# Near products of a chunked scan with a compact output matrix of 64 columns, spread into the padded one by ScalarE

## The chip, the cores and the metric

The kernel runs on one core of one Trainium2 chip, in one launch. The metric is the device time of that execution in microseconds (us); shorter is better. Five engines work side by side, each with its own list of instructions: TensorE (PE in the profile, its weight loads PEld), VectorE (DVE), ScalarE (ACT), GpSimd (POOL) and SyncE (SP), which here only starts DMAs. They wait for each other through semaphores, counters that an instruction raises when it ends and that another engine waits on.

## What is computed

A trunk of two layers on 256 tokens of width 2048, all in float32. Layer 1 is a forgetting attention with a projection before and behind it and is not touched. Layer 0 runs a state-space group (S5) and a differential attention side by side on one projection:

```
h = rms(x, e_norm);  u, z_s5, q, k, v, z_da = split(h @ e_w_in)
# S5: 64 groups of 16 channels, each with 64 complex states
xr, xi = einsum('blgh,gph->blgp', u, B)            # into the states
h_t = a * h_(t-1) + x_t                            # associative_scan over 256 tokens
y = einsum(h_re, c_re) - einsum(h_im, c_im) + d*u
y = gelu(y);  y_s5 = y * sigmoid(y @ w_glu + b_glu) * silu(z_s5)
y_da = diff_attention(q, k, v) * silu(z_da)
x = x + concat(y_s5, y_da) @ e_w_out
```

## The kernel before, in words

**Projections.** Weights stream from memory in units of two 128-row blocks by 512 columns, through a ring of four buffers. To keep float32 accuracy at the fast rate of the float32r type, ACT copies each unit `raw` into a rounded high part `wh` (split_hi, L942), DVE forms the rest `wl` (split_lo, L950), and TensorE multiplies high by high, low by high and high by low (rows_unit, L452 to L454, 12 products of 512 columns per unit). split_hi of a unit waits until TensorE has used the unit four before it (unit_used), split_lo for hi_done, TensorE for lo_done.

**Order.** The order on each engine is written out in the source. The 16 units of two column chunks make a step of slots 0 to 15. In a slot every engine first does the S5 operations and the attention operations assigned to it by the tables of slot numbers at the top of the file, and then (TensorE: before them) its part of the unit; ACT and DVE work three units ahead (LEAD). S5 is done in four batches i = 0 to 3 of 16 groups; slot 0 of batch i is the first slot of step i+1, and negative slots reach back into the step before. The attention of head pair i-1 runs in the same step. Slots below are those of the batch.

**The scan.** The 256 tokens are cut into chunks of HOP = 4. Within a chunk everything is done by a small matrix per tile (a tile is two groups, TB = 8 tiles per batch); between chunks 64 states are carried by a hardware scan on DVE.
- s5_powers (DVE) fills `ba`: B times powers of a. s5_far (DVE, slots -6 and -1, one call for each part r) fills `ca`: C times powers of a, five powers k of 32 output columns. Two groups share a tile: rows 0 to 63 hold group 0 and rows 64 to 127 group 1. `ca` is a padded matrix: group g has its 16 columns at 16g of every 32, and the others are zeros, written once at the start (by POOL's memset, semaphore zeros). Products L1607 (two of 128x640), then L1614 adds or subtracts them half by half into `ca`, and L1618 raises ca_done.
- s5_skip (DVE) fills diag_d, the diagonal of d, with 128 columns.
- s5_turn (TensorE, slot 0) transposes `ba` (L663), and ACT copies it out (L1034, xin_sb).
- s5_near (TensorE, slots 0 and 4, h = 0 and 1): four tiles each, three products into 32 rows of a PSUM bank: L675 and L676 multiply 32 columns of `ba` by 128 columns of `ca` (real and imaginary part), L677 adds the diagonal over 32 columns. It waits for xin_sb, and with h = 0 for ca_done and dd_done. Then ACT (s5_near, slots 1 and 5, L1045) copies the result into `near` four times, each time shifted into another 32 rows (near_sb).
- s5_in_x (TensorE, slots 3 and 6, L691) brings the inputs in, rotate_in and rotate_out (DVE, slots 4, 5 and 8) turn and scan, s5_out_near and s5_out_y (TensorE, slots 7 and 9, L698 and L706, y_ps) form the outputs, and ACT's s5_gelu (L1054, slots 10, 11, 11 and 13) takes them out.

**The attention beside it.** Scores L520 (TensorE) of one head and component wait for sc_max, which DVE (score_in, L1764 to L1767) raises once it has read the scores before them. ACT's exponentials L1176 follow, DVE combines, TensorE transposes (L533, slot 4), ACT copies out (L1184, pt_sb, slot 5) and TensorE multiplies by the values (L546 to L548, slot 5). In a slot, S5 comes ahead of the attention on every engine.

Of the kernel before, what the change touches and what calls it, by code (L numbers as in the profile page):

```python
# [11 lines left out]
ALU = mybir.AluOpType  # L12
# [3 lines left out]
P = 128  # L16
# [57 lines left out]
IN_SLOT, OUT_SLOT = [4, 8], [5, 8]  # L74
GELU_SLOT, HIGH_SLOT = [10, 11, 11, 13], 14
# [51 lines left out]
def build(nc, d, out_dram):  # L127
    ctx = ExitStack()
    with ctx:
# [52 lines left out]
        def small_at(a, n):  # L182
# [26 lines left out]
        g_half = small_at(166, 2)  # L209

# [14 lines left out]
        diag_d = carve("scr", 2, P)  # L225
        used["scr"] += 256
# [33 lines left out]
        ca_t = [flat[:, 3072 + 640 * k:3072 + 640 * (k + 1)].rearrange("p (i k h) -> p i k h", i=TB, k=5)  # L260
                for k in range(2)]
        ba_t = [x.rearrange("p r n -> p (r n)").rearrange("p (i s h) -> p i s h", i=TB, s=HOP) for x in prod]
        phc = carve("scr", 4, GP + 2)
        with nc.sbuf_tensor("mg", [P, TB, NCH], F32) as mg:
# [46 lines left out]
        ba_done, ca_done, dd_done, steps_done = (sem(n) for n in  # L311
            ("ba_done", "ca_done", "dd_done", "steps_done"))
# [120 lines left out]
        def _(pe):  # L433
# [232 lines left out]
            def s5_near(i, h):  # L666

                pe.wait_ge(xin_sb, 4 * i + (3 + h))
                if h == 0:
                    pe.wait_ge(ca_done, i + 1)  # L670
                    pe.wait_ge(dd_done, i + 1)
                o = (xb, yb)[h]
                for e in range(TH):
                    t, at = TH * h + e, e * P
                    nc.tensor.matmul(o[0:32, at:at + P], ba[:, 0, t, 0:32], ca[:, 0, t, 0:P], start=True, stop=False)  # L675
                    nc.tensor.matmul(o[0:32, at:at + P], ba[:, 1, t, 0:32], ca[:, 1, t, 0:P], start=False, stop=False)  # L676
                    mm = nc.tensor.matmul(o[0:32, at:at + 32], ident[:, 32 * e:32 * e + 32],  # L677
                                          diag_d[:, h, 32 * e:32 * e + 32], start=False, stop=True)
                mm.then_inc(near_ps, 1)
# [21 lines left out]
            def s5_out_y(i, h):  # L701
                pe.wait_ge(h_done, 2 * i + (h + 1))
                for e in range(TH):
                    t = TH * h + e
                    for r in range(2):
                        mm = nc.tensor.matmul(xb[:, t * NCH + 1:(t + 1) * NCH], ca[:, r, t, 32:32 + P],  # L706
                                              hst[h][:, r, e * NCH:(e + 1) * NCH - 1], start=False, stop=r == 1,
                                              skip_group_check=True)
                if h:
                    mm.then_inc(y_ps, 1)  # L710
# [244 lines left out]
        def _(act):  # L955
# [81 lines left out]
            def s5_near(i, h):  # L1037

                act.wait_ge(near_ps, 2 * i + (h + 1))
                if h == 0:  # L1040
                    act.wait_ge(y_ps, i) if i else act.wait_ge(zeros, 2)
                src = (xb, yb)[h][0:32, :].rearrange("p (i n) -> p i n", i=TH)
                for s in range(HOP):
                    at = 32 * (HOP - 1 - s)
                    ins = nc.scalar.activation(near[32 * s:32 * s + 32, TH * h:TH * h + TH, at:P], src[:, :, 0:P - at], ACT.Copy)  # L1045
                ins.then_inc(near_sb, 1)

# [13 lines left out]
            def s5(n, s):  # L1061

                for i in range(DA_PAIRS):
                    at = s5_at(n, s, i)
                    if TAB_SLOT[1] + 1 == at:
                        table(i)
                    for k in range(4):
                        if T_SLOT[k] + 1 == at:
                            s5_turned(i, k)
                    for h in range(2):  # L1070
                        if NEAR_SLOT[h] + 1 == at:
                            s5_near(i, h)
                    for k in range(HOP):
                        if GELU_SLOT[k] == at:
                            s5_gelu(i, k)
                    if HIGH_SLOT == at:
                        s5_high(i)
# [347 lines left out]
        def _(dve):  # L1425
# [126 lines left out]
            def gains():  # L1552
# [4 lines left out]
                v.tensor_scalar(g_qk[1][:, 0:1], g_qk[1][:, 0:1], float(HD) ** -0.5, None, ALU.mult)  # L1557
                link(v.memset(g_half, 0.0))
# [36 lines left out]
            def s5_far(i, r):  # L1595
# [13 lines left out]
                times(ca_t[0], r, 0)  # L1609
                link(times(ca_t[1], 1 - r, 1))  # L1610
                for half in range(2):
                    at = slice(64 * half, 64 * half + 64)
                    o = ca[at, r, :, :].rearrange("p i (k h) -> p (i k) h", k=5)[:, :, 16 * half:16 * half + 16]
                    ins = v.tensor_tensor(o, *(x[at].rearrange("p i k h -> p (i k) h") for x in ca_t),  # L1614
                                          ALU.subtract if r else ALU.add)
                link(ins)
                if r:
                    v.memset(junk1[:, 2:3], 0.0).then_inc(ca_done, 1)  # L1618
# [30 lines left out]
            def s5_skip(i):  # L1649
                if i:  # L1650
                    dve.wait_ge(near_ps, 2 * i)
                for c in range(2):
                    ins = v.tensor_scalar(diag_d[:, c, :], ident, d_col[:, 2 * i + c:2 * i + c + 1], None, ALU.mult)
# [7 lines left out]
            def rotate_in(i, h):  # L1661
                dve.wait_ge(x_ps, 2 * i + (h + 1))
                if h == 0:
                    dve.wait_ge(tab_done, i + 1)
                    dve.wait_ge(y_ps, i)
                a1, a2 = prod
# [9 lines left out]
            def rotate_out(i, h):  # L1676
                a1, a2 = prod
# [459 lines left out]
```

## Time and profile before

| | us |
|---|---|
| median of 3 runs | 985.17 (984.67 to 985.78) |
| the profiled execution | 983.37 |
| its span | 981.6 |
| TensorE busy | 966.3 (98% of the span) |
| TensorE weight loads | 828.8 (84%) |
| DVE busy | 629.2 (64%) |
| ACT busy | 572.5 (58%) |
| POOL busy | 94.4 (10%) |

The four batches of the scan lie between about 111 and 370 us of the span. TensorE ran at its full granted clock throughout. A matmul's row in the timeline shows its start and a modelled end; the time that one costs in a stream is the distance from start to start. "Idle before" names the releaser that came last by the profile, which need not be the one that was waited for when an instruction waits for several.

### The profile page before, as it was taken

The page shows a single profiled execution, that of the slowest core. Times are in us where ns is not written, and L with a number is a line of the kernel's source. Part 1 is how long each engine was busy: PE and PEld are TensorE (multiplying, and loading weights), DVE is VectorE, ACT ScalarE, POOL GpSimd, SP SyncE. Part 2 cuts the span into 40 slices and gives each one's busy share as a digit, 9 for nine tenths or more (in the row PEclk, how much of TensorE's full clock was granted, in tenths as well). Part 3 has the DMA queues.
Part 4 walks back from the last instruction along what each step waited for, and adds up shares of the span by engine and source line. Part 5 has one row for each costly group of instructions (what it writes and reads, how often), then busy time and mean ns, then how long its engine had stood idle before and what let it go on. Part 6 is the DMA issues. An engine that isn't in the chain of part 4 may idle for free.

```text
span 981.6 us, 14482 instructions
## 1 busy us (share of the span) xinstructions
PE 966.3 (98%) x5315; PEld 828.8 (84%) x5315; DVE 629.2 (64%) x995; ACT 572.5 (58%) x934; POOL 94.4 (10%) x92
## 2 busy tenths in 40 slices
PE   8999999999999999999999999999999999999998
PEld 7988888788787999888888888888888888888887
DVE  5687898898889755665554654555455545555553
ACT  5697758767567655654445465446545654565332
POOL 2101002011021010000002200220022002200000
PEclk9999999999999999999999999999999999999999
DMA  8874444334433447565799985667999956654662
GB/s 287 207 205 151 151 134 135 119 107 129 141 110 117 129 129 264 166 202 188 173 168 175 168 180 166 177 184 151 173 155 175 196 163 177 180 167 151 215 215 86
DMA packets 113858, 163.63 MB, mean 167 GB/s; under 512 B 19221, under 2 KB 54154, under 8 KB 113546
## 3 DMA queue, kind: packets, MB, share of 16 engines
q1 hardware_dynamic: 99504, 159.67, 61.7%
q10 hardware_dynamic: 14298, 3.22, 1.6%
q8 instruction: 35, 0.57, 0.2%
q14 instruction: 21, 0.17, 0.1%
HBM read 160.76 MB, written 2.10 MB: 166 GB/s over the span
## 4 chain that ended last, share of the span: by engine, by line
PE 90%; DVE 5%; ACT 4%; issue 1%; DMA 0%; SPq 0%; ACTq 0%
PE bank L452 22%; PE bank L454 22%; PE bank L453 22%; PE bank L479 4%; PE bank L480 4%; PE bank L481 4%; ACT uz L1054 2%; PE bank L706 1%; PE bank L691 1%; ACT wh L942 1%; DVE wl L950 1%; PE bank L595 1%; PE bank L520 1%; PE bank L586 1%; PE bank L698 1%
## 5 line engine op out<-in xcount | busy, mean ns | idle before, releaser
L950 DVE TENSOR_TENSOR wl<-raw,wh 128x1024 fp32r<-128x1024 f32 x295 | 361.1, 1228 | 273.0 <-ACT wh L942 271.8
L942 ACT ACTIVATE wh<-raw 128x1024 fp32r<-128x1024 f32 x295 | 310.1, 1057 | 170.0 <-PE bank L454 124.6
L452 PE MATMUL bank<-wh,xh 128*128 128x512 f32 x768 | 309.1, 403 | 0.0
L454 PE MATMUL bank<-wh,xl 128*128 128x512 f32 x768 | 300.3, 391 | 0.0
L453 PE MATMUL bank<-wl,xh 128*128 128x512 f32 x768 | 299.2, 390 | 0.0
L454 PEld LDWEIGHTS bank<-wh,xl 128*128 128x128 f32 x768 | 144.1, 188 | 31.7
L453 PEld LDWEIGHTS bank<-wl,xh 128*128 128x128 f32 x768 | 144.7, 188 | 26.9
L452 PEld LDWEIGHTS bank<-wh,xh 128*128 128x128 f32 x768 | 144.5, 188 | 27.0 <-DVE wl L950 0.2
L452 PE MATMUL bank<-wh,yh 128*128 128x512 f32 x256 | 100.7, 393 | 1.4 <-ACT scr L1345 1.4
L454 PE MATMUL bank<-wh,yl 128*128 128x512 f32 x256 | 99.8, 390 | 0.0
L453 PE MATMUL bank<-wl,yh 128*128 128x512 f32 x256 | 99.6, 389 | 0.0
L479 PE MATMUL bank<-xh,wh 128*128 128x256 f32 x256 | 74.7, 292 | 0.0
L480 PE MATMUL bank<-xl,wh 128*128 128x256 f32 x256 | 72.9, 285 | 0.0
L481 PE MATMUL bank<-xh,wl 128*128 128x256 f32 x256 | 72.8, 285 | 0.0
L452 PEld LDWEIGHTS bank<-wh,yh 128*128 128x128 f32 x256 | 48.1, 188 | 11.3 <-ACT scr L1345 1.6
L454 PEld LDWEIGHTS bank<-wh,yl 128*128 128x128 f32 x256 | 48.0, 188 | 10.2
L453 PEld LDWEIGHTS bank<-wl,yh 128*128 128x128 f32 x256 | 48.1, 188 | 9.6
L2072 POOL TENSOR_TENSOR con<-con 128x4 f32<-128x4 f32 x16 | 22.1, 1378 | 303.6 <-DVE con L1841 303.1
L479 PEld LDWEIGHTS bank<-xh,wh 128*128 128x128 f32 x256 | 49.6, 194 | 0.1
L480 PEld LDWEIGHTS bank<-xl,wh 128*128 128x128 f32 x256 | 49.6, 194 | 0.0
L481 PEld LDWEIGHTS bank<-xh,wl 128*128 128x128 f32 x256 | 49.5, 194 | 0.0
L1054 ACT ACTIVATE uz<-bank 32x128 f32<-32x128 f32 x64 | 25.2, 393 | 13.8 <-PE bank L706 13.0
(326 smaller groups left out, 1107.2 us busy)
## 6 DMA issues: line engine op xcount, KB each, us to landing
raw<-in_o_w_in SPq DMA_DIRECT2D x128, 512.0 KB
raw<-in_e_w_in SPq DMA_DIRECT2D x130, 256.0 KB, 3.2
raw<-in_e_w_out SPq DMA_DIRECT2D x32, 512.0 KB
raw<-in_o_w_out SPq DMA_DIRECT2D x32, 512.0 KB
raw<-in_e_w_in SPq DMA_DIRECT2D x31, 512.0 KB
raw<-in_s_w_glu SPq DMA_DIRECT2D x8, 512.0 KB
res<-in_x SPq DMA_DIRECT2D x8, 256.0 KB, 6.9
res<-in_x SPq DMA_DIRECT2D x1, 2048.0 KB, 10.1
```

Of the source, the lines that this page charges most:

```text
L452: nc.tensor.matmul(o, l_hi, w_hi, start=first, stop=False)
L453: nc.tensor.matmul(o, l_hi, w_lo, start=False, stop=False)
L454: mm = nc.tensor.matmul(o, l_lo, w_hi, start=False, stop=last)
L479: nc.tensor.matmul(o, w_hi, rh[:, kt, :], start=first and n % 2 == 0, stop=False, skip_group_check=True)
L480: nc.tensor.matmul(o, w_hi, rl[:, kt, :], start=False, stop=False, skip_group_check=True)
L481: mm = nc.tensor.matmul(o, w_lo, rh[:, kt, :], start=False, stop=last, skip_group_check=True)
L520: mm = nc.tensor.matmul(scb[:, o:o + w], s_sb[:, 2 * h + comp, t * P:(t + 1) * P], qkt[:, h, 1, 0:w], start=True, stop=True)
L586: mm = nc.tensor.transpose(trb[:, b * T + t * P:b * T + (t + 1) * P], x[:, t, h * HD:(h + 1) * HD], ident)
L942: nc.scalar.activation(wh[:, j % RING, :], raw[:, j % RING, :], ACT.Copy).then_inc(hi_done, 1)
L950: nc.vector.tensor_tensor(wl[:, j % RING, :], raw[:, j % RING, :], wh[:, j % RING, :].bitcast(F32), ALU.subtract).then_inc(lo_done, 1)
L1054: ins = nc.scalar.activation(dst[:, :, :, k], src[:, :, q, :], ACT.Gelu_apprx_tanh)
L2072: link(g.tensor_tensor(rnn[:, m:m + 4], ssn[:, m:m + 4], expo[:, m:m + 4], ALU.pow))
```

## The change

The near products read a compact matrix `cc[r]` (128 rows; 8 tiles, 5 powers, 16 columns) in place of the padded `ca`: both groups of a tile lie in the same 16 columns, so a product has 64 columns instead of 128, and the diagonal 16 instead of 32. The output for a tile row is thus the same 64 columns whichever group the row belongs to.
- **DVE**: s5_far writes its result in one operation into `cc[r]` and raises cc_done; it no longer writes `ca`. diag_d has 16 columns per half. At the start, gains() gets three reductions: `ident16` (a 128x16 identity pattern) and `of_group`, two columns of ones and zeros by group. rotate_in and rotate_out get waits for near_ps and ca_done, because `cc` lies in memory that they write.
- **ACT**: a new s5_pad(i, r), slots -4 and 1 (PAD_SLOT), copies `cc[r]` into the padded `ca`, 64 rows at a time, and raises ca_done. s5_near now makes eight copies in place of four: for each shift and each group g one copy of half the size, in runs of 16 columns, with the scale `of_group[:, g]`, which leaves the rows of the other group zero.
- **TensorE**: s5_near waits for cc_done in place of ca_done; ca_done is waited for in s5_out_y, the only other reader of `ca`.

No slot of another operation is changed.

```diff
+PAD_SLOT = [-4, 1]
@@ TensorE, s5_near
                 if h == 0:
-                    pe.wait_ge(ca_done, i + 1)
+                    pe.wait_ge(cc_done, 2 * i + 2)
                     pe.wait_ge(dd_done, i + 1)
                 o = (xb, yb)[h]
                 for e in range(TH):
-                    t, at = TH * h + e, e * P
-                    nc.tensor.matmul(o[0:32, at:at + P], ba[:, 0, t, 0:32], ca[:, 0, t, 0:P], start=True, stop=False)
-                    nc.tensor.matmul(o[0:32, at:at + P], ba[:, 1, t, 0:32], ca[:, 1, t, 0:P], start=False, stop=False)
-                    mm = nc.tensor.matmul(o[0:32, at:at + 32], ident[:, 32 * e:32 * e + 32],
-                                          diag_d[:, h, 32 * e:32 * e + 32], start=False, stop=True)
+                    t, at = TH * h + e, e * 64
+                    for r in range(2):
+                        nc.tensor.matmul(o[0:32, at:at + 64], ba[:, r, t, 0:32],
+                                         cc[r][:, t, 0:HOP, :].rearrange("p k h -> p (k h)"), start=r == 0, stop=False)
+                    mm = nc.tensor.matmul(o[0:32, at:at + 16], ident[:, 32 * e:32 * e + 32],
+                                          diag_d[:, h, :], start=False, stop=True)
@@ TensorE, s5_out_y
+                if h == 0:
+                    pe.wait_ge(ca_done, i + 1)
@@ ACT, s5_near
+                    act.wait_ge(group_done, 1)
-                src = (xb, yb)[h][0:32, :].rearrange("p (i n) -> p i n", i=TH)
+                src = (xb, yb)[h][0:32, 0:256].rearrange("p (i k c) -> p i k c", i=TH, k=HOP)
                 for s in range(HOP):
-                    at = 32 * (HOP - 1 - s)
-                    ins = nc.scalar.activation(near[32 * s:32 * s + 32, TH * h:TH * h + TH, at:P], src[:, :, 0:P - at], ACT.Copy)
+                    dst = near[32 * s:32 * s + 32, TH * h:TH * h + TH, :].rearrange("p i (k g c) -> p i k g c", k=HOP, g=2)
+                    for g in range(2):
+                        ins = nc.scalar.activation(dst[:, :, HOP - 1 - s:HOP, g, :], src[:, :, 0:s + 1, :], ACT.Copy,
+                                                   scale=of_group[0:32, g:g + 1])
                 ins.then_inc(near_sb, 1)
+            def s5_pad(i, r):
+                act.wait_ge(cc_done, 2 * i + (r + 1))
+                if r == 0:
+                    act.wait_ge(y_ps, i) if i else act.wait_ge(zeros, 2)
+                for g in range(2):
+                    at = slice(64 * g, 64 * g + 64)
+                    dst = ca[at, r, :, :].rearrange("p i (k h) -> p (i k) h", k=5)[:, :, 16 * g:16 * g + 16]
+                    ins = nc.scalar.activation(dst, cc[r][at].rearrange("p i k h -> p (i k) h"), ACT.Copy)
+                if r:
+                    ins.then_inc(ca_done, 1)
@@ DVE, gains
+                v.tensor_reduce(ident16, ident.rearrange("p (a h) -> p h a", h=16), AX.X, ALU.add)
+                link(v.tensor_reduce(quarter, ident.rearrange("p (a h) -> p a h", h=16), AX.X, ALU.add))
+                v.tensor_reduce(of_group, quarter.rearrange("p (q g) -> p g q", g=2), AX.X, ALU.add).then_inc(group_done, 1)
@@ DVE, s5_far
-                times(ca_t[0], r, 0)
-                link(times(ca_t[1], 1 - r, 1))
-                for half in range(2):
-                    at = slice(64 * half, 64 * half + 64)
-                    o = ca[at, r, :, :].rearrange("p i (k h) -> p (i k) h", k=5)[:, :, 16 * half:16 * half + 16]
-                    ins = v.tensor_tensor(o, *(x[at].rearrange("p i k h -> p (i k) h") for x in ca_t),
-                                          ALU.subtract if r else ALU.add)
-                link(ins)
-                if r:
-                    v.memset(junk1[:, 2:3], 0.0).then_inc(ca_done, 1)
+                times(cc[r], r, 0)
+                link(times(ca_t, 1 - r, 1))
+                flat_of = "p i k h -> p (i k h)"
+                v.tensor_tensor(cc[r].rearrange(flat_of), cc[r].rearrange(flat_of), ca_t.rearrange(flat_of),
+                                ALU.subtract if r else ALU.add).then_inc(cc_done, 1)
+                dve.wait_ge(cc_done, 2 * i + (r + 1))
@@ DVE, s5_skip
-                    ins = v.tensor_scalar(diag_d[:, c, :], ident, d_col[:, 2 * i + c:2 * i + c + 1], None, ALU.mult)
+                    ins = v.tensor_scalar(diag_d[:, c, :], ident16, d_col[:, 2 * i + c:2 * i + c + 1], None, ALU.mult)
@@ DVE, rotate_in (h = 1) and rotate_out (h = 0)
+                    dve.wait_ge(near_ps, 2 * i + 2)
+                    dve.wait_ge(ca_done, i + 1)
```

How the lists change at three places. TensorE around the near products of batch 0, slot 0; before (scr holds `ba` and diag_d, res holds `ca`, con the identity, bank is PSUM):

```order
L663 MATMUL bank<-con,scr 128x128 x3
L675 MATMUL bank<-res,scr 32x128 [waits dd_done,ca_done,xin_sb]
L676 MATMUL bank<-res,scr 32x128
L677 MATMUL bank<-scr,con 32x32
L675 MATMUL bank<-res,scr 32x128
L676 MATMUL bank<-res,scr 32x128
L677 MATMUL bank<-scr,con 32x32
```

and now (`cc` lies in scr too):

```order
L666 MATMUL bank<-con,scr 128x128 x3
L679 MATMUL bank<-scr 32x64 [waits dd_done,cc_done,xin_sb]
L679 MATMUL bank<-scr 32x64
L681 MATMUL bank<-scr,con 32x16
L679 MATMUL bank<-scr 32x64 x2
L681 MATMUL bank<-scr,con 32x16
```

The same products stand in the same place with half the columns; the scores (L520, now L523) still follow them. ACT in slot 1 of batch 0, from the copies of `near` to the next split; before:

```order
L1045 ACTIVATE res<-bank 32x4x32 [waits zeros,near_ps]
L1045 ACTIVATE res<-bank 32x4x64
L1045 ACTIVATE res<-bank 32x4x96
L1045 ACTIVATE res<-bank 32x512
L1176 ACT_TABLE_LOAD
L1176 ACTIVATE scr,con<-scr,con 128x128 [waits sc_max]
L1176 ACTIVATE scr,con<-scr,con 128x256
L942 ACTIVATE wh<-raw 128x1024 [waits unit_used,raw_in0]
```

and now:

```order
L1053 ACTIVATE res<-bank,con 32x4x16 [waits group_done,zeros,near_ps]
L1053 ACTIVATE res<-bank,con 32x4x16
L1053 ACTIVATE res<-bank,con 32x4x2x16 x2
L1053 ACTIVATE res<-bank,con 32x4x3x16 x2
L1053 ACTIVATE res<-bank,con 32x16x16 x2
L1065 ACTIVATE res<-scr 64x40x16 [waits cc_done]
L1065 ACTIVATE res<-scr 64x40x16
L1199 ACT_TABLE_LOAD
L1199 ACTIVATE scr,con<-scr,con 128x128 [waits sc_max]
L1199 ACTIVATE scr,con<-scr,con 128x256
L948 ACTIVATE wh<-raw 128x1024 [waits unit_used,raw_in0]
```

Four copies more and the two of s5_pad(0, 1) stand ahead of the first exponentials and of the split. DVE at slot -1 of batch 0, from s5_far(0, 1) to the scores' maxima; before:

```order
L1607 TENSOR_TENSOR scr<-early,res 128x640 x2
L1614 TENSOR_TENSOR res<-scr 64x40x16 [waits dve_link]
L1614 TENSOR_TENSOR res<-scr 64x40x16
L1618 MEMSET con 128x1 [waits dve_link]
L950 TENSOR_TENSOR wl<-raw,wh 128x1024 [waits hi_done]
L1764 SCALAR_TENSOR_TENSOR scr<-con,bank 128x384 [waits sc_ps]
```

and now:

```order
L1633 TENSOR_TENSOR scr<-early,res 128x640 x2
L1638 TENSOR_TENSOR scr<-scr 128x640 [waits dve_link]
L956 TENSOR_TENSOR wl<-raw,wh 128x1024 [waits hi_done,cc_done]
L1792 SCALAR_TENSOR_TENSOR scr<-con,bank 128x384 [waits sc_ps]
L1794 TENSOR_REDUCE con<-scr 128x1 [waits dve_link]
```

Three instructions have become one ahead of the split; cc_done there is DVE's own. The rest keeps its place.

## Rows read from the trace of the kernel before

**Rows 1.** The page: busy time, share of the span and instructions of each engine.
```profile
PE 966.3 (98%) x5315; PEld 828.8 (84%) x5315; DVE 629.2 (64%) x995; ACT 572.5 (58%) x934; POOL 94.4 (10%) x92
```

**Rows 2.** The page: the chain that ended last, shares by engine.
```profile
PE 90%; DVE 5%; ACT 4%; issue 1%; DMA 0%; SPq 0%; ACTq 0%
```

**Rows 3.** Timeline of TensorE, batch 1: start, us, engine, line, operation [idle before].
```profile
181.50 0.38 PE L675 MATMUL bank<-res,scr 128*32 128x128 f32 x2 [1.20 <-ACT scr L1034]
...
182.00 0.39 PE L675 MATMUL bank<-res,scr 128*32 128x128 f32 x2
...
182.44 0.23 PE L677 MATMUL bank<-scr,con 128*32 128x32 f32 x2
182.50 0.39 PE L675 MATMUL bank<-res,scr 128*32 128x128 f32 x2
...
183.88 0.92 PE L520 MATMUL bank<-scr 128*128 128x256 f32 x4 [0.23 <-DVE con L1767]
```

**Rows 4.** The chain in order of time, 156 to 184.5 us: start, us, what.
```profile
156.66 0.38 issue
...
168.10 1.23 DVE wl L950
...
181.34 0.06 DVE con L1618
...
183.84 0.04 issue
```

**Rows 5.** The chain in order of time, TensorE in batches 0 and 1.
```profile
126.10 1.73 PE bank L691 x16
127.83 0.71 PE bank L520 x4
...
195.42 0.71 PE bank L520 x4
```

**Rows 6.** Groups by line and form: xcount | busy us, mean ns | idle before.
```profile
L942 ACT ACTIVATE wh<-raw 128x1024 fp32r<-128x1024 f32 x295 | 310.1, 1057 | 170.0 <-PE bank L454 124.6 <-PE bank L481 20.1 <-DMA raw<-in_o_w_in 11.8
L1054 ACT ACTIVATE uz<-bank 32x128 f32<-32x128 f32 x64 | 25.2, 393 | 13.8 <-PE bank L706 13.0
L675 PE MATMUL bank<-res,scr 128*32 128x128 f32 x64 | 12.4, 276 | 3.8 <-ACT scr L1034 3.8
L1034 ACT ACTIVATE scr<-bank 128x512 f32<-128x512 f32 x16 | 8.6, 589 | 2.3 <-PE bank L663 2.3
L1148 ACT ACTIVATE scr<-scr 128x512 f32<-128x512 f32 x8 | 5.0, 627 | 0.6 <-DVE con L1753 0.5
L1045 ACT ACTIVATE res<-bank 32x512 f32<-32x512 f32 x8 | 4.7, 587 | 0.1
L1135 ACT ACTIVATE scr<-bank,con 128x512 f32<-128x512 f32 x4 | 2.8, 688 | 6.7 <-PE bank L454 6.7
L1045 ACT ACTIVATE res<-bank 32x128 f32<-32x128 f32 x8 | 2.1, 267 | 27.7 <-PE bank L677 27.7
```

**Rows 7.** Timeline of ACT, batch 2: two splits in a row, four copies of near.
```profile
257.05 1.99 ACT L942 ACTIVATE wh<-raw 128x1024 fp32r<-128x1024 f32 x2
...
268.61 1.74 ACT L1045 ACTIVATE res<-bank 32x128 f32<-32x128 f32 x4 [4.36 <-PE bank L677]
```

**Rows 8.** Groups by line and form, DVE in s5_far.
```profile
L1614 DVE TENSOR_TENSOR res<-scr 64x640 f32<-64x640 f32 x16 | 13.1, 820 | 0.4
L1607 DVE TENSOR_TENSOR scr<-early,res 128x640 f32<-128x640 f32 x16 | 12.4, 817 | 0.0
```

**Rows 9.** Timeline of DVE: a split at the start, the maxima of batches 0, 1.
```profile
52.38 1.23 DVE L950 TENSOR_TENSOR wl<-raw,wh 128x1024 fp32r<-128x1024 f32 x1 [1.04 <-ACT wh L942]
...
126.27 0.41 DVE L1767 TENSOR_REDUCE con<-scr 128x1 f32<-128x256 f32 x1
...
193.57 0.41 DVE L1767 TENSOR_REDUCE con<-scr 128x1 f32<-128x256 f32 x1
```

**Rows 10.** Timeline of all engines, 266 to 272.5 us: the probabilities to the values.
```profile
271.27 0.47 ACT L1184 ACTIVATE scr<-bank 128x384 f32<-128x384 f32 x1
...
271.79 0.49 PE L546 MATMUL bank<-scr 128*128 128x128 f32 x2
```

More of the change, by code:

```diff
@@ L209, in build @@
         g_half = small_at(166, 2)
+        quarter = small_at(168, 8)
+        of_group = small_at(176, 2)
+        ident16 = small_at(178, 16)
         qk = carve("scr", NT, CW)
@@ L224, in build @@
         ba = carve("scr", 2, TB, HOP * 32)
-        diag_d = carve("scr", 2, P)
-        used["scr"] += 256
+        diag_d = carve("scr", 2, 16)
+        used["scr"] += 480
         main1 = used["scr"]
@@ L259, in build @@
         bt = [flat[:, 4096 + 512 * k:4608 + 512 * k].rearrange("p (a h) -> p a h", a=GP) for k in range(2)]
-        ca_t = [flat[:, 3072 + 640 * k:3072 + 640 * (k + 1)].rearrange("p (i k h) -> p i k h", i=TB, k=5)
-                for k in range(2)]
+        ca_t, *cc = [flat[:, at:at + 640].rearrange("p (i k h) -> p i k h", i=TB, k=5) for at in (3072, 3840, 4480)]
         ba_t = [x.rearrange("p r n -> p (r n)").rearrange("p (i s h) -> p i s h", i=TB, s=HOP) for x in prod]
@@ L310, in build @@
         u4_done, slopes = sem("u4_done"), sem("slopes")
-        ba_done, ca_done, dd_done, steps_done = (sem(n) for n in
-            ("ba_done", "ca_done", "dd_done", "steps_done"))
+        ba_done, cc_done, ca_done, dd_done, steps_done, group_done = (sem(n) for n in
+            ("ba_done", "cc_done", "ca_done", "dd_done", "steps_done", "group_done"))
         t_ps, xin_sb, near_ps, near_sb, x_ps, x_read, h_done, y_ps = (sem(n) for n in
@@ L1070, in s5 @@
                     for h in range(2):
+                        if PAD_SLOT[h] == at:
+                            s5_pad(i, h)
                         if NEAR_SLOT[h] + 1 == at:
@@ L1665, in rotate_in @@
                     dve.wait_ge(y_ps, i)
+                else:
+                    dve.wait_ge(near_ps, 2 * i + 2)
+                    dve.wait_ge(ca_done, i + 1)
                 a1, a2 = prod
@@ L1676, in rotate_out @@
             def rotate_out(i, h):
+                if h == 0:
+                    dve.wait_ge(near_ps, 2 * i + 2)
+                    dve.wait_ge(ca_done, i + 1)
                 a1, a2 = prod
```

## The prediction

> **What bounds the kernel now.** I read the page's busy table first: TensorE is busy for 966.3 us of a span of 981.6 us [rows 1], and the chain that ended last lies 90% on it, with DVE 5% and ACT 4% [rows 2]. So a microsecond taken off TensorE counts if nothing else ends late in its place, and the next question is where, among the scan's steps, that 9% on other engines sits. The profiled execution took 983.37 us as a whole (span 981.6), 1.8 under the median of 985.17. I work out a difference in the profiled execution and add it to the median.
>
> Next the timeline of TensorE around the near products of batch 1. Before L675 it idles 1.20 us, named after ACT; before the second scores product, L520, it idles 0.23 us, named after DVE [rows 3]. The first name misleads. s5_near also waits for ca_done, and the chain shows DVE's L1618, which signals ca_done, at 181.34 to 181.40, 0.1 us before L675 begins. The same chain is ACT and DVE without a gap from the end of the scan's output products (156.66) through the split at 168.10 to L520 at 183.88 [rows 4]. This is the most important row of the page: for 27.2 us in each of batches 1 to 3 TensorE is only just ahead of a chain of ACT and DVE, and the change puts work on ACT.
>
> **TensorE's part.** A tile of the near product is L675, L676 and L677; each fp32 product is two instructions. From 182.00 to 182.50 one tile takes 0.50 us: 0.22 for each pair of 128 columns, 0.06 for the pair of 32 columns (182.44 to 182.50) [rows 3]. So 110 ns for 128 columns and 30 ns for 32. With 64 columns I take 55 ns, so 0.11 for a pair. The last product (16 columns) I leave at 0.06. A tile then takes 0.28, a call of four tiles 0.88 less, and eight calls (64 instructions of L675 [rows 6] are two per tile, four tiles per call) 7.0 us less. The bound from the other side is L691: 16 instructions with 64 columns take 1.73 us, 108 ns each [rows 5], as long as 128 columns. There 128 weight columns are loaded, here 32, and L677 shows that a load of 32 columns fits into 30 ns; so I take 55.
>
> By the Trainium skill ("TensorE: Matmul & The Clock Gate", LDWEIGHTS (loading the stationary operand)) a load costs time by its columns, about columns / 1.2 ns, whatever the rows. That would be 107 ns for L691 and 27 for the near products, so 55 would stand and the sum with it. The two rows agree with the page.
>
> **ACT's part.** s5_near: now four copies of 128, 256, 384 and 512 elements, 1.74 us in a row [rows 7]; the shortest takes 267 ns and the longest 587, so 160 ns and 0.83 per element [rows 6]. Afterwards there are eight, two each of 64, 128, 192 and 256: 2 x (0.213 + 0.267 + 0.320 + 0.374) = 2.35. Each takes its scale from a column in memory; that costs 0.10 us (L1135 with it 688, L1034 without 589, same shape [rows 6]), so 0.79 more. With 0.06 between them it is 3.20, a growth of 1.45 us per call.
> s5_pad: two copies of 64x640 out of SBUF. L942 (1024 elements) takes 1057 ns and L1148 (512) 627 [rows 6], so 640 take 0.735 and the two 1.47 us, in two calls per batch.
> Do neighbours overlap? Two L942 take 1.99, 0.12 less than twice 1.057; four L1045 take 1.74, no less than the sum of 1.71 that the same line gives [rows 7]. The new ones are the latter kind (part of the partitions), so I take them one after another and keep 0.1 per instruction for the range.
> Writes in runs of 16 elements: L1614 does this on DVE at 820 ns, and L1607 without runs takes 817 [rows 8]: no price. The upper bound is L1054, which writes every fourth element: 393 ns for 128 elements against 267 [rows 6], 1 ns more per element.
>
> **DVE's part.** s5_far: two L1614 in a row, 0.82 each, and the L1618 that follows become one operation of 128x640, priced as L1607 at 0.82: 0.95 less before the signal. s5_skip gets shorter off the path. The three reductions in gains() stand ahead of the split at 52.38, which idled 1.04 us for ACT [rows 9]. They are two of 128 elements and one of 16, and L1767 takes 0.41 for 256 [rows 9], so together they stay under 1 us and hide in it; without that cover they would cost up to 1.0. The new DVE waits in rotate_out and rotate_in ask for near_ps and ca_done. In stage B below DVE gets 2.6 us later and TensorE's near products 0.9 earlier, so both are met by then. On SP and POOL nothing moves.
>
> **Where it lands.** Stage A, from the output products of batch i-1 to L520 of batch i, three times. s5_pad(i, 0) stands on ACT in front of a split that the chain runs through: +1.47; DVE gives back 0.95. TensorE cannot cash its 0.88, because it waits for cc_done and then for sc_max anyway. L520 comes 0.52 later. What is queued behind the pad is two splits, the last GELU and the transposed inputs.
> Stage B, from the first near product to the third slot's L520 (fourth score). It waits for sc_max, which DVE reaches through ACT's near copies, exponentials and split. sc_max now ends at 126.68 and 193.98, and L520 begins at 127.83 and 195.42 [rows 5, 9]: 1.1 and 1.4 us of slack. ACT now begins 0.88 earlier, then has 1.45 + 1.47 more. Batch 0: -0.88 + 2.92 = +2.04, so 128.72 + 0.04 against 127.83, which is +0.93. Batches 1 to 3: 0.52 - 0.88 + 2.92 = +2.56, so 196.58 against 195.42, +1.16 with stage A in it.
> Stage C, the second near product to L546. L546 begins at 271.79, 0.05 after ACT's L1184 ends (271.27 + 0.47) [rows 10]; no slack. ACT begins 0.88 earlier and ends 1.45 later: +0.57, four times.
> Sum: 0.93 + 0.57 + 3 x (1.16 + 0.57) = 6.7 us. The profiled execution would be 990.1, the median 985.17 + 6.7 = **991.9 us**.
>
> **Rivals.**
> 1. The gain of TensorE arrives: 985.17 - 7.0 = 978.1. For it: 90% of the chain on TensorE. Against it: L520 and L546 begin 0.04 and 0.05 us after their releasers. It decides in stage C: if the near copies grow by less than 0.88, the stage gains, and if the pads hide too, all does. It would need an ACT whose added copies cost nearly nothing.
> 2. The new copies overlap as L942 does. If the two copies into the same 32 partitions do, by 0.1 four times, the growth is 1.05 in place of 1.45: batch 0 gives 0.53 + 0.17, the others 0.76 + 0.17, in all 3.5, so 988.7. If all of them and the pads overlap, growth is 0.75, the pad 1.37 and the sum 0.4: 985.6. For it L942, against it L1045, whose copies go to four different quarters, which these pairs do not.
> The Trainium skill ("ScalarE: Activation LUTs", What ACT_TABLE_LOAD costs) has 186 ns plus 0.833 per element, 93 more for each pointer operand, and 93 of overlap between neighbours. The pointer's price agrees with [rows 6], L942's overlap roughly with [rows 7], but the four L1045 there do not overlap. By the page the growth would be 1.12, the pad 1.25 and the sum 2.5.
> 3. The products get no shorter (108 ns as L691): every 0.88 goes. Batch 0 then loses 1.81 + 1.45 and the others 2.04 + 1.45: 13.7, so 998.9. Against it L677's 30 ns.
> 4. Runs of 16 cost as L1054's writes: 0.63 per pad copy and 1.26 per near call, 25.6 in all, 1010.8. Against it L1614.
>
> **How the numbers follow.** Forecast 0.50, its own range 990 to 994; rival 2 0.26, half of which ends within 0.2% (983.2 to 987.1, about what three runs can tell from no change); rival 3 0.08, rival 4 0.07, rival 1 0.09 with a little of it within 0.2%. So faster 0.08, same 0.13, slower 0.79. The range of 986 to 998 leaves out rivals 1, 3 and 4 and the far end of rival 2.
>
> **What would show it.** In the profile after: L679 in a tile of about 0.28 us; L1053 x8 at about 3.2 us and L1065 x2 at 1.5; waits of TensorE at L523 (scores) for DVE, above 1 us for the second or the fourth, and at L549 (values) for ACT of about 1.6 us, four times each. A part of stage A's wait can show at the transposes L508, which the same chain feeds. TensorE's busy time falls by about 7 while the span grows. I am wrong if L549 waits less than 0.9 us (then copies overlap), or if L523 does not wait.

## The result: 3.4 us slower, half of the forecast

The changed kernel takes 988.12 us (median of 8 runs, 987.32 to 988.85), the kernel before 984.74 in the same comparison (8 runs, 983.63 to 985.78). The ratio is 1.0034, 95% interval 1.0025 to 1.0043. The forecast was 991.9 and +6.7 us: the sign was right, the size double.

The profiled run's span is 986.4 us, 4.8 longer than that of before; 1.2 of the 4.8 lie ahead of the scan and are not the change (experiments 7 and 8). The busy table of after, columns as in [rows 1]:

```profile
PE 961.4 (97%) x5315; PEld 823.3 (83%) x5315; DVE 623.0 (63%) x986; ACT 591.4 (60%) x982; POOL 92.4 (9%) x92
```

TensorE is busy for 4.9 us less, where the forecast said about 7 (more on this under stage B below), and ACT for 18.9 us more. The chain of after, shares of the span, against [rows 2]:

```profile
PE 88%; ACT 6%; DVE 5%; issue 1%; DMA 1%; SPq 0%; DVEq 0%; ACTq 0%
```

TensorE's waits, all of the run (for what, us in total, times, longest):

```profile
PE bank L523 <- DVE con L1795: 5.0, 6, 1.4
PE bank L549 <- ACT scr L1207: 3.6, 4, 0.9
PE bank L740 <- DMA scr<-in_e_norm: 3.4, 1, 3.4
PE bank L508 <- DVE scr L1788: 3.2, 3, 1.1
PE bank L666 <- ACT scr L1040: 2.1, 4, 0.7
PE bank L750 <- DMA res<-in_x: 1.9, 2, 1.6
```

L523 (scores), L549 (values) and L508 (transposes) wait where the forecast said; L549 for 0.93 us in batches 0 to 2 and 0.81 in batch 3, where it had 1.6. TensorE in batch 1, against [rows 3]:

```profile
184.04 0.38 PE L679 MATMUL bank<-scr 128*32 128x64 f32 x4 [0.24 <-ACT scr L1040]
184.26 0.21 PE L681 MATMUL bank<-scr,con 128*32 128x16 f32 x2
184.32 0.39 PE L679 MATMUL bank<-scr 128*32 128x64 f32 x4
186.43 0.92 PE L523 MATMUL bank<-scr 128*128 128x256 f32 x4 [1.09 <-DVE con L1795]
198.15 0.92 PE L523 MATMUL bank<-scr 128*128 128x256 f32 x4 [0.19 <-DVE con L1795]
207.24 0.49 PE L549 MATMUL bank<-scr 128*128 128x128 f32 x2 [0.93 <-ACT scr L1207]
```

A tile is 0.28 us (184.04 to 184.32), as forecast; near(0) now waits for the transposed inputs, not for the right operand. ACT at the same place, and its instructions by form (count, busy us, mean ns), against [rows 7] and [rows 6]:

```profile
185.37 2.67 ACT L1053 ACTIVATE res<-bank,con 32x64 f32<-32x64 f32 x8 [0.93 <-PE bank L681]
188.07 1.49 ACT L1065 ACTIVATE res<-scr 64x640 f32<-64x640 f32 x2
```
```profile
L1065 ACT ACTIVATE res<-scr 64x640 f32<-64x640 f32 x16 | 11.8, 736 | 0.2
L1053 ACT ACTIVATE res<-bank,con 32x256 f32<-32x256 f32 x16 | 6.6, 456 | 0.1
L1053 ACT ACTIVATE res<-bank,con 32x192 f32<-32x192 f32 x16 | 5.7, 402 | 0.1
L1053 ACT ACTIVATE res<-bank,con 32x128 f32<-32x128 f32 x16 | 4.9, 350 | 0.1
L1053 ACT ACTIVATE res<-bank,con 32x64 f32<-32x64 f32 x16 | 4.0, 297 | 13.1 <-PE bank L681 13.1
```

The pads are what was forecast (736 ns each, 1.49 the pair). The eight near copies are not: the forms add up to 2 x (0.297 + 0.350 + 0.402 + 0.456) = 3.01, but a call takes 2.67 or 2.68. The chain shows where the difference is, pair by pair (start, length, what):

```profile
185.37 0.50 ACT res L1053 x2
185.88 0.61 ACT res L1053 x2
186.50 0.71 ACT res L1053 x2
187.23 0.82 ACT res L1053 x2
```

Two copies of 297 ns are done after 0.50: the neighbours that write the same 32 partitions overlap by 0.09. So a call grew by 2.68 - 1.74 = 0.94, not by 1.45. The two of a pair also have the same shape and read the same elements. Equal shape alone does not do it: the two pads, of one shape, write different halves of the partitions and take 1.49 for twice 736 ns, and so it is with the GELU's copies of before, four of one shape to four quarters, 1.60 for 4 x 393 ns:

```profile
156.63 1.60 ACT L1054 ACTIVATE uz<-bank 32x128 f32<-32x128 f32 x4 [2.87 <-PE bank L706]
```

**By stages.** How much later each place is in after than in before, from the two timelines of TensorE, in us:

| | batch 0 | 1 | 2 | 3 |
|---|---|---|---|---|
| near(0) begins | 1.18 | 2.54 | 3.60 | 4.68 |
| fourth score (L520, L523) | 1.82 | 2.89 | 3.97 | 4.68 |
| values (L546, L549) | 1.96 | 3.03 | 4.09 | 4.77 |

Down a column B is row two less row one, C is row three less row two, and A leads to the next column (the second values product is at 1.97, 3.02 and 4.10). A: 0.57, 0.58, 0.58. B: 0.64, 0.35, 0.37, 0.00. C: 0.14, 0.14, 0.12, 0.09. Together 3.6 us, beside a start that is 1.2 later; the medians, 3.4 apart, agree with the 3.6.

### The profile page after: what moved, and what is told of

It reads as the page before. It is cut to its first block, busy times and chain, and to the rows that moved or that the text cites. A ratio compares the mean times of both kernels' runs of the same rounds, so it can differ in the third digit from the quotient of the medians.

```text
span 986.4 us, 14541 instructions
## 1 busy us (share of the span) xinstructions
PE 961.4 (97%) x5315; PEld 823.3 (83%) x5315; DVE 623.0 (63%) x986; ACT 591.4 (60%) x982; POOL 92.4 (9%) x92
## 4 chain that ended last, share of the span: by engine, by line
PE 88%; ACT 6%; DVE 5%; issue 1%; DMA 1%; SPq 0%; DVEq 0%; ACTq 0%
PE bank L455 22%; PE bank L457 22%; PE bank L456 21%; PE bank L482 4%; PE bank L483 4%; PE bank L484 4%; ACT res L1053 2%; ACT wh L948 1%; PE bank L712 1%; DVE wl L956 1%; PE bank L598 1%; PE bank L695 1%; PE bank L523 1%; ACT res L1065 1%; PE bank L589 1%
## 5 line engine op out<-in xcount | busy, mean ns | idle before, releaser
L1296 ACT ACTIVATE scr<-bank,con 128x256 f32<-128x256 f32 x32 | 13.4, 471 | 32.3 <-PE bank L589 32.3
```

The costliest lines, as they stand in the source:

```text
L1296: ins = nc.scalar.activation(qkt[:, h % 2, b, :], trb[:, b * T:(b + 1) * T], ACT.Copy, scale=g_qk[1][:, b:b + 1])
```

## Experiments

Kernels timed together shared their runs of before: 984.99 us for experiments 1 to 4, 984.39 for 5 to 8, 984.30 for 9 and 10; these medians of one kernel, 984.74 of the result among them, differ by up to 0.7 us, and a distance to the changed kernel (988.12, timed apart from the experiments) is no better known than that. "Changed kernel" is the one that the prediction is about.

**1. The pads on GpSimd.** Taken from ACT's program, and put into GpSimd's behind qk_norm(i, 1), with `pad` making the same two copies.

```diff
-                        if PAD_SLOT[h] == at:
-                            s5_pad(i, h)
...
+                    for r in range(2):
+                        pad(i, r)
```

> The pad copies are taken from ACT and given to GpSimd, in the same order of batches. Theory (ACT's pads lie on the path in stages A and B, 2 x 1.49 us per batch, and the near copies' growth of about 0.94 there just eats TensorE's 0.88): without them L523 of the fourth score no longer waits in any batch, DVE's 0.95 in stage A arrives in part, and the time falls by 5 to 7 us against the changed kernel, to 981 to 983, which is under the kernel before. Rival (the pads hide and the loss comes from the near copies or from DVE's new waits): the time stays at 988 within 1. A second rival (GpSimd's copies slow DVE down while they run): 984 to 987, with DVE's operations near 95 and 165 us longer than in the changed kernel.

Measured: 981.69 us, ratio to before 0.9969 (0.9957 to 0.9981), 6.4 less than the changed kernel and faster than before. GpSimd takes 1.23 us for each pad copy, off the path. The three largest waits of TensorE over the run:

```profile
PE bank L549 <- ACT scr L1205: 3.6, 4, 0.9
PE bank L740 <- DMA scr<-in_e_norm: 3.6, 1, 3.6
PE bank L523 <- DVE con L1793: 3.2, 3, 1.1
```

L508's waits are gone and L523 waits three times, not six; L549 is untouched. Against before, stage A is now 0.93 shorter each time (DVE's 0.95), stage B of batch 0 0.85 shorter (TensorE's 0.88), stage C still 0.07 to 0.11 longer. The pads carried all the loss of A and B. In batches 1 to 3 stage B is as long as before and no shorter: there the second score waits 1.05 to 1.09 us for DVE, which takes up TensorE's 0.88. DVE's L1631 kept its 817 ns beside GpSimd, so the second rival falls too.

**2. Products of 128 columns again.**

```diff
-                                         cc[r][:, t, 0:HOP, :].rearrange("p k h -> p (k h)"), ...
+                                         cc[r].rearrange("p i k h -> p (i k h)")[:, at:at + P], ...
```

> Only TensorE's part is undone: the near products have 128 columns again (the right operand is a 128-column window of the compact matrix, so the values are not the reference's), all else as in the changed kernel. Theory (the 0.88 us per call arrives in full, because ACT's copies start that much earlier in each of the eight calls): a tile takes 0.51 in place of 0.29, and the time rises by 8 x 0.88 = 7.0, to 995. Rival (TensorE waits there for ACT and DVE whatever the products take, so their shortening was worth nothing): 988 to 989.

The right operand is a window of the compact matrix, so the shapes are those of 128 columns and the values are not the reference's; the near copies read the output with that spacing. Measured: 997.09 us (4 runs, 995.54 to 999.18), 9.0 above the changed kernel. The profiled spans differ by 9.8: a start 1.5 later, the products' 8 x 0.85 = 6.8, and some 1.6 from a clock that fell once (last section). So, with ACT's chain as it is in the changed kernel, the shortening of the products had arrived in full in all eight calls, as the theory had it, though a further 2 us of the median were not foreseen.

**3. The same eight copies in another order.**

```diff
-                for s in range(HOP):
-                    dst = ...
-                    for g in range(2):
+                for g in range(2):
+                    for s in range(HOP):
+                        dst = ...
```

> The eight near copies in another order: all four of group 0, then all four of group 1, so that neighbours no longer write the same 32 partitions. Theory (two copies in a row into the same 32 partitions overlap by 0.09 us, four times per call, and this is most of why the growth was 0.94 and not 1.45): L1053 x8 takes 3.0 to 3.1 in place of 2.68, and since each call is on the path the time rises by 8 x 0.36 = 2.9, to 991. Rival (the copies are cheaper for another reason, and their order is nothing): x8 stays at 2.68 and the time at 988.

Measured: 993.26 us, ratio 1.0085 (1.0071 to 1.0099), 5.1 above the changed kernel. ACT's timeline and one of its four forms:

```profile
187.91 3.17 ACT L1053 ACTIVATE res<-bank,con 32x64 f32<-32x64 f32 x8 [0.93 <-PE bank L681]
```
```profile
L1053 ACT ACTIVATE res<-bank,con 32x64 f32<-32x64 f32 x16 | 4.9, 306 | 14.8 <-PE bank L681 14.7
```

The copies are the same; a call takes 3.17, close to the 3.20 of the prediction. That is 0.49 more and not the 0.36 expected: besides the 0.09 of overlap per pair there is now about 0.01 between the two, and the second copy is 0.02 longer. Stages B and C are 0.44 to 0.52 longer each, 3.9 us in all; another 1.6 of the profiled execution is the clock again. One execution with a mean clock of 1.000 took 992.50. This run decides the cause: without the overlap the change would have cost 3.6 + 3.9 = 7.5 us, against 6.7 forecast.

**4. Four copies in place of eight.** The inner loop over g runs once.

```diff
-                    for g in range(2):
+                    for g in range(1):
```

> Only the four near copies of group 0 are made; the other group's columns stay zero, so the output is not the reference's. Theory (the near copies are on the path in every call): x4 takes 1.5 us, 1.2 less than the eight, stage C gains it up to the next late release, and the time falls by 5 to 6, to 982 to 983. Rival (only the pads are on the path): no more than 1 us less, 987 to 988.

It leaves out group 1's half of the near matrix. Measured: 983.63 us, ratio 0.9985 (0.9976 to 0.9994), 4.5 less than the changed kernel for 8 x 1.11 taken from ACT (four copies take 1.57). L549 no longer waits, and stage C is 1.0 to 1.2 shorter. Stage B is 1.1 shorter in batch 0, 0.4 in batches 1 and 2, where the fourth score had waited 0.2, and the same in batch 3, where it had not waited. Between the first and the second values product 1.5 us come back in all, 1.0 of it in batch 0, where L536 (the transposes of the probabilities) waits 0.8 us for DVE. The near copies are on the path in seven of the eight calls, but only as deep as those waits.

**5. Copies as before, masked by GpSimd; tiles interleaved.** The output of the near products, the weights of the output products, and GpSimd's mask:

```diff
+                    out = o[0:32, 0:256].rearrange("p (z i) -> p z i", i=TH)[:, :, e]
...
-                    nc.tensor.matmul(xb[...], near[:, t, :], ...)
+                    nc.tensor.matmul(xb[...], near[:, t // TH, :, t % TH], ...)
...
+                g.tensor_tensor(x, x, y, ALU.mult).then_inc(near_ok, 1)
```

> A candidate: pads on GpSimd as in e1_pad_pool, and the near copies without a group scale. ACT makes four unmasked copies of 128, 256, 384 and 512 elements (each column block read twice, once per group), as in the kernel before; GpSimd then multiplies the matrix with the group mask in one 128x512 operation per call, off ACT. For that the four tiles lie interleaved, one element every 16 bytes, in the products' output and in the weights of L703. Theory (TensorE's 0.88 per call arrives once ACT's part of the near copies is no longer than before): L1053's line takes 1.74 in place of 2.68, so stages B and C gain 0.9 per call as far as DVE's next release allows; 2 to 5 us under the 981.7 of e1_pad_pool, 977 to 980. Rival (interleaved writes or weights cost TensorE more than 55 ns per product, or GpSimd's mask comes late for the output products): 982 to 990, with the tile of the near product above 0.35 us or a wait of TensorE at L703.

Measured: 987.78 us. ACT's part did what the theory said (1.74), the products kept their 0.28 a tile, but the output products with weights at one element every 16 bytes doubled. Here, then the same 16 instructions with contiguous weights (experiment 9):

```profile
145.08 3.72 PE L703 MATMUL bank<-early,res 128*128 128x64 f32 x16
```
```profile
145.38 1.89 PE L702 MATMUL bank<-early,res 128*128 128x64 f32 x16
```

That is 4 x 1.83 = 7.3 us; with it off, 987.78 would be 980.5, half a microsecond above the 977 to 980 expected, and the profiled execution lost another 1.6 to the clock. The rival was right on its first half.

**6. The eight copies without their scale.**

```diff
-                        ... ACT.Copy, scale=of_group[0:32, g:g + 1])
+                        ... ACT.Copy)
```

> The eight near copies without their scale from memory (so the groups are not masked and the output is not the reference's). Theory (the pointer costs 0.10 us per instruction as L1135 against L1034 showed): each form is 0.10 shorter, x8 takes 1.8 to 1.9, and since the near copies are on the path until the next release is late (four copies, 1.1 us shorter per call, gave 4.5 in all), the time falls by 3 to 5, to 983 to 985. Rival (the pointer costs nothing in such short copies): x8 at 2.68, 988.

It leaves out the mask that keeps the groups apart. Measured: 984.94 us, 3.2 less than the changed kernel. Two of the forms:

```profile
L1053 ACT ACTIVATE res<-bank 32x256 f32<-32x256 f32 x16 | 5.1, 365 | 0.1
L1053 ACT ACTIVATE res<-bank 32x64 f32<-32x64 f32 x16 | 2.5, 205 | 14.5 <-PE bank L681 14.5
```

297 - 205 and 456 - 365: the scale costs 0.09 us per instruction, 0.73 per call (2.68 to 1.95). The prediction's 0.10 stands.

**7. The kernel before, profiled again.** No edit.

> The kernel before once more, for a second profile. The profiled run of before reached its first scan products 1.2 us earlier than the profile of the changed kernel and than those of its variants, and the first products of the input waited 1.04 us for their data against 1.6 to 2.6 there. Theory (that is the scatter of the start from run to run and no part of the change): this profile can start as late as the others, with all later distances between stages of batches 0 to 3 equal to the first profile within 0.1 us; the time 984 to 986. Rival (the 1.2 us belong to the change, by its reductions in the setup): the start comes where it did before.

Measured: 983.95 us. Where the two profiles of before, and the changed kernel, begin near(0) of batch 0:

```profile
114.18 0.41 PE L675 MATMUL bank<-res,scr 128*32 128x128 f32 x2 [0.20 <-ACT scr L1034]
```
```profile
115.36 0.41 PE L679 MATMUL bank<-scr 128*32 128x64 f32 x4 [0.19 <-ACT scr L1040]
```

The second profile of before has it at 114.9, and experiment 8, which holds all of the change, at 113.8; from there the two of before keep their distances. So the start scatters by more than the 1.2 in question, with the wait for the inputs (L744, L750: 0.7 to 2.7 us over the profiles). The part of the change in the setup is small: from the start of the split before the reductions to the start of the split behind them DVE takes 3.47 us in the changed kernel and 3.45 before, and still idles 0.37 there for ACT (before 1.04).

**8. DVE's saving undone.**

```diff
                 link(times(ca_t, 1 - r, 1))
+                link(times(ca_t, 1 - r, 1))
```

> Only DVE's saving is undone: each half of s5_far repeats one product of 128x640 (the same values), 0.82 us more before cc_done, close to the 0.95 that the change took out. Theory (stage A's chain of ACT and DVE sets the end in batches 1 to 3, and DVE's 0.95 arrives there in full; it arrives nowhere else): the time rises by 3 x 0.85 = 2.5, to 990.7, with near(0) of batches 1 to 3 each 0.8 us later against the batch before and the steps from near(0) to the values unchanged. Rival (DVE's part is off the path, the pads' 1.5 alone makes stage A): 988.

In the profiled execution (989.06 us) stage A takes 0.88, 0.84 and 0.84 longer than in the changed kernel, together 2.6, and B and C are as they were. TensorE's waits show the place:

```profile
PE bank L679 <- ACT scr L1040: 3.5, 4, 1.1
```

against 0.9 us in all in the changed kernel. DVE's term is right. But the median of its 4 runs is 993.37, not the 990.7 expected: the three others took 993.2 to 994.1, with a mean granted clock of 0.995 to 0.998.

**9. Eight copies without scale, masked by GpSimd, weights contiguous.**

```diff
+                x = near[:, TH * h:TH * h + TH, :].rearrange("p i (k g c) -> p (i k) g c", g=2, c=16)
+                g.tensor_tensor(x, x, y, ALU.mult).then_inc(near_ok, 1)
```

> The candidate mended: pads on GpSimd, eight near copies without a scale into the matrix as it lies in the changed kernel (weights contiguous), and the group mask by one GpSimd multiplication of 128x512 per call. e5_mask_pool showed that the interleaved weights cost L703 3.72 us in place of 1.89 and that nothing else went wrong there. Theory: L1053's line takes 1.95 as in e6_no_scale, L702 x16 1.89, and the waits of TensorE at L549 (0.9 us, four times in e1_pad_pool) shrink by up to 0.73 each: 2.9 under e1_pad_pool, 979, if DVE's next release (L536) does not take it back; at least 980.5. Rival (ACT's part of the near copies is no longer what is late once the pads are gone): 981.7 as e1_pad_pool.

Measured: 979.32 us, ratio 0.9951 (0.9937 to 0.9964): 5.0 us under before, 8.8 under the changed kernel. Nothing is left out of the computation. TensorE's waits, all of the run:

```profile
PE bank L740 <- DMA scr<-in_e_norm: 3.4, 1, 3.4
PE bank L523 <- DVE con L1791: 3.0, 3, 1.1
PE bank L455 <- ACT scr L1364: 1.4, 1, 1.4
PE bank L750 <- DMA res<-in_x: 1.3, 2, 1.0
PE bank L666 <- ACT scr L1040: 1.0, 4, 0.3
PE bank L679 <- ACT scr L1040: 0.8, 4, 0.2
PE bank L536 <- DVE scr L1805: 0.6, 1, 0.6
PE bank L549 <- ACT scr L1203: 0.6, 3, 0.2
```

L549 waits 0.6 us in all in place of 3.6. Less than the 3.0 arrives (2.4 against experiment 1), since L536 waits in batch 0. Where the gain against before lies, by the two timelines: stage A 2.6 us (DVE's saving), stage B 1.1 (0.9 of it in batch 0), stage C 2.7, and 1.2 come back between the first and the second values product. So half of it is DVE's one operation in place of two, and TensorE's 0.88 still goes into the second score's wait in batches 1 to 3.

**10. Experiment 8 once more, for a long execution.** No further edit.

> e8_dve_more once more, for a profile of one of its longer executions. Its profiled run took 989.1 with the chain 2.6 us longer, as the theory had it, but three others took 993.2 to 994.1 at a mean granted clock of 0.995 to 0.998. Theory (as in e2_prod128 and e3_g_outer, where a TensorE wait of over 1.7 us in batch 0 or 1 was followed by some 3 us at a granted clock of 0.5): this profile shows one to three such stretches, each behind one of the waits at L523 and each worth about 1.6 us. Rival (the added DVE work is worth more than 2.6 us on the path in most runs): the distances between stages grow by over 0.9 with the clock at 1.0.

Measured: 989.54 us at a mean clock of 0.999, so again a short one. It repeats experiment 8's stage A (0.85, 0.84 and 0.84 longer than in the changed kernel) and tells nothing of the long ones; what they did stays unseen. The expectation has a wait "of over 1.7 us" ahead of the clock's fall in both experiments 2 and 3; the rows show 1.84 in experiment 3 and 1.04 in experiment 2 (last section).

## Why the forecast was right in sign and wrong in size

With 0.94 for the growth, and nothing else changed, the forecast's own arithmetic gives 0.42 + 3 x (0.52 + 0.13) + 4 x 0.06 = 2.6 us, where the two timelines show 3.6. So one mis-sized term made the forecast 4.1 too large, and 1.0 was missing elsewhere.

- **TensorE's part**, 0.88 a call: right (tile 0.28; 0.85 a call in experiment 2).
- **ACT's part** failed, in one term: "With 0.06 between them it is 3.20, a growth of 1.45 us per call." Durations (297 to 456 ns against 313 to 474 priced with the scale) and scale were near, but the eight copies were taken one after another. The pairs overlap, a call takes 2.68 and grows by 0.94. Four neighbours in [rows 7] write four different quarters and do not overlap; the forecast carried that over to pairs that write one quarter. Rival 2 had named it, with 0.26 and 988.7. Its mechanism was right; that its time comes within 0.6 of the measured 988.12 is in part luck: its growth of 1.05 was 0.11 too large, and what it lacked is told under stage B. Experiment 3 shows that it is the order of the copies. The Trainium skill ("ScalarE: Activation LUTs", What ACT_TABLE_LOAD costs) states an overlap of about 93 ns between neighbours without that condition: the pairs agree with 0.09, while the copies of other quarters in experiment 3 lie about 10 ns apart.
- **The pads**: right (1.49), on the path in A and B (experiment 1).
- **DVE's part**: right; 0.95 arrives in stage A only (experiments 1 and 8). The setup's reductions hide.
- **Stage A**: forecast 0.52 three times, measured 0.57 to 0.58.
- **Stage B**: forecast 0.93 and 3 x 0.64, measured 0.64, 0.35, 0.37 and 0.00. With growth 0.94 the arithmetic gives 0.42 and 0.13. Batch 1 shows what is missing: ACT begins 1.33 after near(0) in place of 2.20 (-0.87), from there to sc_max 2.45 are added (0.94 + 1.49), and 1.41 of slack goes, which is +0.17 of the 0.19 that the starts of L520 and L523 on the chain and the timeline show (195.42 and 198.15). The table's 0.35 takes L520's start from the timeline (195.26), where it stands 0.16 before the end of the products ahead of it; behind an idle, as in the changed kernel, both views agree. But the whole loss is real: the second near product begins 17.31 us after the first one before and 17.73 now, +0.42. On the chain the fourth score lasts 0.71 us in a stream [rows 5] and 0.92 behind the idle:

```profile
198.15 0.92 PE bank L523 x4
```

  So a wait costs some 0.2 us more than its idle, and the forecast had priced it as the idle alone. Experiment 4 agrees: with L549's idle of 0.93 gone, the stretch from the second near product to the values is 1.08 shorter. The ten further idles of TensorE between 110 and 350 us, at 0.2 each, would also be the 2 us by which its busy time fell less than 7; that is an estimate. In batch 3 the kernel before takes 14.15 us from near(0) to the fourth score, against 13.76 in batches 1 and 2; with this 0.39 more slack L523 does not wait and nothing is lost. The forecast had taken the three batches as alike.
- **Stage C**: forecast 0.57 four times, measured 0.09 to 0.14; with 0.94 it is 0.94 - 0.88 = 0.06. Counted as the forecast did, from the second near product to the values, it grew by 0.07 in every batch. More than half of the error is here: 2.28 forecast, 0.49 measured.
- Of the signs listed, "wrong if L549 waits less than 0.9 us (then copies overlap)" came out at 0.93, on the edge, and the copies did overlap. The sign was badly set: L549's wait follows the growth of the copies (growth 0.94, wait 0.93; 0.21 and 0.19 in experiment 6; 1.43 and 1.41 in experiment 3), so the forecast's 1.45 meant a wait of 1.45, not 1.6, and rival 2's 1.05 would not have passed below 0.9 either. TensorE's waits at L523 came as forecast, one above 1 us in each batch.

## What to carry to other kernels

Where work moves from a busy engine to one that feeds it, price the moved instructions in the order in which they will stand: in this kernel the same eight copies cost 2.68 or 3.17 us by order alone. Ask of every new operation which engine has nobody waiting: pads and mask on ACT turned the change into a loss, and on GpSimd, which is slower at the copy (1.23 us against 0.74), they cost nothing (experiments 1 and 9). Even then TensorE's gain did not arrive in all eight calls: where the next wait is for DVE, only DVE's own saving counts. And of two variants with equal sums, look at how far the compact layout forces the readers of it into strides (experiment 5).

## What the hardware showed that I had not expected

**TensorE's clock fell in the middle of the kernel.** In experiment 3 TensorE idles 1.84 us before the fourth score of batch 0. The stretches around it (length, PE busy, granted clock, DMA share, GB/s):

```profile
128.00:129.99 1.99, 0.15 (x2) 1.00 0.46 145
129.99:131.00 1.01, 1.01 (x5) 0.96 0.94 294
131.00:134.00 3.00, 3.00 (x8) 0.50 0.74 238
134.00:136.00 2.00, 2.00 (x21) 0.91 0.01 4
```

For 3.4 us the granted clock is 0.50, the lower of its levels (1.2 GHz in place of 2.4), which costs 1.6 us: from the fourth score to the values batch 0 takes 1.6 more than the other batches do against the changed kernel. In experiment 2 the same follows an idle of 1.04 us in batch 1:

```profile
202.20 1.46 PE L523 MATMUL bank<-scr 128*128 128x256 f32 x4 [1.04 <-DVE con L1795]
```
```profile
200.00:202.00 2.00, 1.16 (x11) 1.00 0.47 160
202.00:203.00 1.00, 0.80 (x2) 0.71 0.91 266
203.00:204.00 1.00, 1.00 (x5) 0.50 0.75 260
204.00:205.00 1.00, 1.00 (x4) 0.50 0.56 138
```

Batch 2 of the same run has the same idle of 1.04 us, and the clock stays at 1.00. In experiment 5 the fall follows the 3.72 us of slow products with no idle at all. In the changed kernel an idle of 1.36 us at the same place of batch 0 left the clock at 1.00. So a longer wait did not always bring the fall, and a wait can cost twice, by its idle and by the clock. The long executions of experiment 8 took 4.2 to 5.1 us more than the profiled one. Their mean clocks of 0.995, 0.997 and 0.998 stand for some 5, 3 and 2 us lost to the clock, worked out as the missing share of 990 us; the first fits, the other two leave 1 to 2 us unexplained, and no profile shows any of them.

**Weights with a stride.** Weights of 128 columns, one element every 16 bytes, cost 232 ns per product in place of 118; the same stride in the products' output in PSUM cost nothing (0.28 us a tile).
